# Prompt attention of a hybrid decoder step: weights divided by their sums before their transposition, the sink of mixer B as a column of logits

## What is computed

```python
def sparse_attend(q, k_sel, v_sel, dist, table):           # mixer A
    logits = einsum('btngd,btjnd->btngj', q, k_sel) * HEAD_DIM ** -0.5 + bias
    logits = where(dist >= 0, logits, NEG)
    p = softmax(logits, axis=-1)
    o = einsum('btngj,btjnd->btngd', p, v_sel)

def sink_softmax(logits, sinks):                            # mixer B
    m = maximum(max(logits, axis=-1, keepdims=True), s)
    e = exp(logits - m)
    return e / (sum(e, axis=-1, keepdims=True) + exp(s - m))
```

## Time and profile before

| | |
|---|---|
| median of 3 runs | 2341.65 us (2341.57 to 2344.51) |
| the profiled execution, its own time | 2343.02 us |
| its span, first to last instruction | 2341.2 us |
| mean granted TensorE clock | 0.982 of full |
| busy in the span | PE 96%, PEld 87%, DVE 49%, ACT 18%, POOL 44% |
| prompt attention of mixer A | about 595 to 727 us of the span |
| prompt attention of mixer B | about 1764 to 1844 us of the span |

### The profile page before, as it was taken

How to read it: one execution, slowest core, us unless ns; L and a number is a source line. 1 busy time by engine, 2 the same in 40 slices (tenths; PEclk the granted TensorE clock), 3 DMA queues, 4 the chain that set the end, 5 groups by cost and what they waited for, 6 DMA issues and landing times.

```text
span 2341.2 us, 39794 instructions
## 1 busy us (share of the span) xinstructions
PE 2258.6 (96%) x14801; PEld 2029.8 (87%) x14819; DVE 1137.1 (49%) x1811; ACT 415.4 (18%) x848; POOL 1029.7 (44%) x622
## 2 busy tenths in 40 slices
PE   7999999999888899999999999999999999999997
PEld 6999989959666588999999999999996689999997
DVE  4544522488584546555512555542264465555311
ACT  3101000131554412010000101000015420101002
POOL 4546455414001024555555555555541055555552
PEclk9999999999799999999999999999999899999998
DMA  5435363535003433333223333322350023333221
GB/s 125 99 73 115 78 155 89 114 64 147 10 1 100 130 89 77 86 81 81 78 84 90 82 86 85 81 78 82 94 154 23 1 73 81 81 86 83 79 83 60
DMA packets 378042, 196.33 MB, mean 84 GB/s; under 512 B 66531, under 2 KB 374476, under 8 KB 377932
## 3 DMA queue, kind: packets, MB, share of 16 engines
q1 hardware_dynamic: 366108, 180.79, 31.3%
q10 hardware_dynamic: 11552, 13.71, 2.0%
q0 software_dynamic: 288, 0.56, 0.1%
HBM read 192.23 MB, written 11.64 MB: 87 GB/s over the span
## 4 chain that ended last, share of the span: by engine, by line
PE 61%; DVE 2%; ACTq 0%; ACT 0%; issue 0%; DVEq 0%
PE psum L594 17%; PE psum L597 11%; PE psum L595 10%; PE psum L593 10%; PE psum L596 9%; PE psum L749 1%; PE psum L775 1%; DVE XS L1448 1%; PE psum L745 1%; PE psum L789 1%; ACTq L1200 0%; PE psum L758 0%; DVE squares L1481 0%; PE psum L939 0%; PE psum L938 0%
## 5 line engine op out<-in xcount | busy, mean ns | idle before, releaser
L545 POOL CAST WSP<-WST 128x1024 fp32r<-128x1024 f32 (+1 forms) x305 | 310.5, 1018 | 1250.0 <-PE psum L597 1008.8
L547 POOL TENSOR_TENSOR WSP<-WST,WSP 128x1024 fp32r<-128x1024 f32 (+1 forms) x305 | 709.3, 2326 | 24.5
L594 PE MATMUL psum<-XS,WSP 128*128 128x512 f32 x1672 | 658.4, 394 | 0.0
L593 PE MATMUL psum<-XS,WSP 128*128 128x320 f32 x1672 | 520.4, 311 | 9.5 <-DVE XS L1448 4.3
L597 PE MATMUL psum<-XS,WSP 128*128 128x320 f32 x1672 | 522.7, 313 | 0.0
L595 PE MATMUL psum<-XS,WSP 128*128 128x320 f32 x1672 | 519.2, 311 | 0.0
L596 PE MATMUL psum<-XS,WSP 128*128 128x256 f32 x1672 | 474.0, 283 | 0.0
L596 PEld LDWEIGHTS psum<-XS,WSP 128*128 128x128 f32 x1672 | 314.8, 188 | 71.5
L593 PEld LDWEIGHTS psum<-XS,WSP 128*128 128x128 f32 x1672 | 321.4, 192 | 11.6 <-DVE XS L1448 5.2
L597 PEld LDWEIGHTS psum<-XS,WSP 128*128 128x128 f32 x1672 | 321.5, 192 | 0.0
L594 PEld LDWEIGHTS psum<-XS,WSP 128*128 128x128 f32 x1672 | 314.4, 188 | 0.4
(11 more groups left out here) (325 smaller groups left out, 2595.0 us busy)
## 6 DMA issues: line engine op xcount, KB each, us to landing
WST<-in_ffn_w_gate SPq DMA_DIRECT2D x168, 256.0 KB, 3.9
WST<-in_ffn_w_up SPq DMA_DIRECT2D x168, 256.0 KB, 3.9
WST<-in_ffn_w_down SPq DMA_DIRECT2D x192, 224.0 KB, 3.5
WST<-in_a_w_in SPq DMA_DIRECT2D x28, 256.0 KB, 4.4
kv0A<-in_cache_kv SPq DMA_DIRECT2D x48, 128.0 KB, 2.3
kv2A<-in_cache_kv SPq DMA_DIRECT2D x48, 128.0 KB, 2.3
WST<-in_b_w_in SPq DMA_DIRECT2D x20, 256.0 KB, 4.0
kscr<-in_cache_idx SPq DMA_DIRECT2D x128, 32.0 KB, 2.1
```

Of the source, the lines that this page charges most:

```text
L545: nc.gpsimd.tensor_copy(WSP[s][:, 0, 0:width], WST[s][:, 0:width]).then_inc(w_hi, 1)
L547: nc.gpsimd.tensor_tensor(WSP[s][:, 1, 0:width], WST[s][:, 0:width], WSP[s][:, 0, 0:width].bitcast(F32), ALU.subtract).then_inc(w_split, 1)
L593: mm(front, high, x[:, 0, 0:FRONT], start=first, stop=False)
L594: mm(split, high, x[:, :, FRONT:TOK], start=first, stop=False)
```

## The change

The weights are divided before they are transposed, so that the products with v need no scaling.

- For each unit VectorE takes the reciprocals of its two sums (`factors(u)`, 128x2), queued behind the maximum of unit u + 1. Then the two halves of `p` are multiplied in place by the row's reciprocal: in mixer A by GpSimd (two TENSOR_SCALAR of 128 x nk, the second behind the first), in mixer B by VectorE itself (two TENSOR_SCALAR). `transposed(u)` waits for these (`pn_set`) instead of for the exponentials.
- `row_scales` of TensorE, `scales` of ScalarE, `products` of VectorE and `otok` are gone. The high part is read from the bank by ScalarE (`high_part`), the low part by VectorE (`low_part`), half a tile at a time, in units g = 5 and 7 of a tile and g = 1 and 3 of the next.
- TensorE's order is now `logits(u + 2)`, `values(u - 1)`, `transposed(u)`.
- In mixer B the strip has two columns more (`STRIP["B"]` = 258): the sink and a masked one. They are added to the logits by the strip's matmuls; maximum and exponentials run over nk + 2 columns, and the sink's own steps (L1602, `es`) go.
- `block_diagonal` of mixer A moves from VectorE behind unit 27 to GpSimd behind unit 1: a memset 128x1024 and two copies of 64 x 512.
- GpSimd waits for the last multiplication, no longer for `qk_ps`, before it splits `outA`. In mixer A's sample attention the keys of sample 0 are transposed ahead of the small products (`new_logits`), and wait only for the bank that they write; in mixer B the first key transpositions wait for no evacuation.

```diff
         def _(pool):
+            def block_diagonal(m, ms):
+                pool.wait_ge(acc_evac, at["inA"][1] + A_CHUNKS + RING)
+                nc.gpsimd.memset(m["qbd"][:, :, :], 0.0).then_inc(ms["qbd_clear"], 1)
...
-            pool.wait_ge(MS["A"]["qk_ps"], NQT * GRP)
+            m, ms = mixers["A"], MS["A"]
+            for u, (i, g) in enumerate((i, g) for i in ORDER["A"] for g in range(GRP)):
+                pool.wait_ge(ms["ri_set"], u + 1)
+                for n in range(KVH):
+                    if u or n:
+                        pool.wait_ge(ms["pn_set"], 2 * u + n)
+                    p = m["p"][:, u % 2, n, 0:key_range("A", i)[1]]
+                    nc.gpsimd.tensor_scalar(p, p, m["ri"][:, i, n, g:g + 1], None, ALU.mult).then_inc(ms["pn_set"], 1)
+                if u == 1:
+                    pool.wait_ge(ms["pn_set"], 4)
+                    block_diagonal(m, ms)
+            pool.wait_ge(MS["A"]["pn_set"], 2 * NQT * GRP)
...
         def _(pe):
-                                 m["ri"][:, i, n, g:g + 1].to_broadcast([P, HD]), ident[:, :], start=True, stop=True)
...
-                        pe.wait_ge(ms["p_set"], 2 * u + n + 1)
+                        pe.wait_ge(ms["pn_set"], 2 * u + n + 1)
...
-                        pe.wait_ge(ms["o_evac"], 2 * (r - 1) + g // 4 + 1)
+                        pe.wait_ge(ms["ot_evac"], 2 * (r - 1) + g // 4 + 1)
...
-                for u, (r, i, g) in enumerate(units):
-                    more = u + 2 < len(units)
-                    transposed(u)
-                    if g == GRP - 1:
-                        row_scales(r, i)
-                    elif more:
+                for u in range(len(units)):
+                    if u + 2 < len(units):
                         logits(u + 2)
                     if u:
                         values(u - 1)
-                    if g == GRP - 1 and more:
-                        logits(u + 2)
+                    transposed(u)
                 values(len(units) - 1)
...
         def _(act):
-                    nk = key_range(L, i)[1]
+                    nk = key_range(L, i)[1] + SINK[L]
...
+                def high_part(r, h):
                     i = ORDER[L][r]
+                    act.wait_ge(ms["pv_ps"], GRP * r + 4 * h + 4)
+                    fn(XH[:, 4 * h:4 * h + 4, i * P:(i + 1) * P], bank[6 + h].rearrange("p (g t) -> p g t", g=4), ACT.Copy)\
+                        .then_inc(ms["oh_set"], 1)
...
         def _(dve):
+                def factors(u):
+                    r, i, g = units[u]
+                    dve.wait_ge(ms["p_set"], 2 * (u + 1))
+                    nc.vector.reciprocal(m["ri"][:, i, :, g], m["rs"][:, i, :, g]).then_inc(ms["ri_set"], 1)
+                    if L == "B":
+                        dve.wait_ge(ms["ri_set"], u + 1)
+                        for n in range(KVH):
+                            p = m["p"][:, u % 2, n, 0:key_range(L, i)[1]]
+                            ts(p, p, m["ri"][:, i, n, g:g + 1], None, ALU.mult).then_inc(ms["pn_set"], 1)
...
+                    nc.vector.tensor_reduce(m["nm"][:, i, :, g], PS[u % 2][:, :, 0:nk], AX, ALU.max, negate=True)\
+                        .then_inc(ms["nm_set"], 1)
+                    if u:
+                        factors(u - 1)
+                    if g == 7:
+                        low_part(r, 0)
                     if g == 3 and r:
-                        parts(r - 1)
+                        low_part(r - 1, 1)
                     after(u)
...
+SINK = {"A": 0, "B": 2}
+STRIP = {L: 2 * P + SINK[L] for L in "AB"}
```

More of the change, by code:

```diff
@@ L1237, in prompt_attention @@
                         exps(u + 1)
-                    if L == "A" and r and g == 2:
-                        high_parts(r - 1)
-                    if L == "B" and g == GRP - 2:
-                        act.wait_ge(ms["es_in"], r + 1)
-                        fn(m["es"][:, :, :], m["es"][:, :, :], ACT.Exp).then_inc(ms["es_set"], 1)
                     nk = key_range(L, i)[1]
@@ L1256, in prompt_attention @@
                     after(u)
-                    if g == GRP - 1:
-                        scales(r)
-                if L == "A":
-                    high_parts(NQT - 1)
+                    if g == 5:
+                        high_part(r, 0)
+                    if g == 1 and r:
+                        high_part(r - 1, 1)
+                high_part(NQT - 1, 1)
             def paged_sample_attention(m, ms):
@@ L1558, in prompt_attention @@
                 units = [(r, i, g) for r, i in enumerate(ORDER[L]) for g in range(GRP)]
-                def row_scales(r):
-                    i = ORDER[L][r]
-                    dve.wait_ge(ms["p_set"], 2 * GRP * (r + 1))
-                    rs, ri = m["rs"][:, i], m["ri"][:, i]
-                    if L == "B":
-                        dve.wait_ge(ms["es_set"], r + 1)
-                        steps.done(tt(rs, rs, m["es"][:, :, :], ALU.add))
-                    nc.vector.reciprocal(ri, rs).then_inc(ms["ri_set"], 1)
@@ L1593, in prompt_attention @@
                         between(r)
[L1594 to L1596 removed]
+                    nk = key_range(L, i)[1] + SINK[L]
                     dve.wait_ge(ms["qk_ps"], u + 1)
[L1598 to L1610 removed]
+                    nc.vector.tensor_reduce(m["nm"][:, i, :, g], PS[u % 2][:, :, 0:nk], AX, ALU.max, negate=True)\
[4 more added lines that the diff above has]
+                        low_part(r, 0)
                     if g == 3 and r:
[L1612 removed]
+                        low_part(r - 1, 1)
                     after(u)
[L1614 to L1616 removed]
+                factors(len(units) - 1)
+                low_part(NQT - 1, 1)
             def paged_sample_attention(m, ms):
```

106 lines of the change are left out of this document (29 added, 77 removed).

## The result

The changed kernel takes 2347.39 us in the median of 20 runs (2340.88 to 2354.71), the kernel before, run between them on the same chip, 2343.3 (2338.27 to 2346.68, 20 runs). The ratio is 1.0021, with a 95% interval of 1.0011 to 1.0031: some 5 us slower, where 2332.5 and a ratio of 0.996 were forecast. The profiled execution of the change took 2354.71 us (span 2352.9) and is the slowest of its 20; stages are therefore compared by their own lengths, not by the two ends.

The account below looks back on a forecast made before the run. TensorE was taken to bound mixer B; mixer A begins as a loop of small steps over several engines. A -0.6, clock +1.5 and B -10.0 made -9.1 us: 2333.9 profiled, 2332.5 us median, range 2327 to 2344.

Parts of the forecast that it names:

- A, to the end of tile 0: Mixer A, tile 0: turns of 4.4 us add 8.8 over seven turns, first transposition 1.2 later: +10.0 us.
- A, tiles 1 and 2: Mixer A: tile ends' row scales go, VectorE's queue is what is left, 57.3 plus 1.5 us against 65.2: -6.4.
- A, tile 3: Mixer A, tile 3: two row-scale groups of 2 us and the last product go, one group counted: -2.0 us.
- A, start of the sample part: Mixer A's sample attention: key transpositions now lie beside the last high and low part: -2.2 us.
- A, clock: Mixer A: TensorE, working a smaller part of tile 0, may get 2.4 GHz a few us later: +1.5 us.
- B, first to last transposition: Mixer B: the extra 2.62 us at each of three tile ends is removed, together 7.9 us.
- B, end of the prompt part: Mixer B, last transposition to first key transposition: 4.06 us falls to 1.0, saving 3.1 us.
- B, fill: Mixer B, first unit: reciprocal and multiplications lack cover once: +1.0 us.
- the 1.3 that the prediction had named as a sign of being wrong: Mixer A: a GpSimd multiplication above 1.3 us for 512 would show the forecast wrong.
- The first rival: Mixer A: GpSimd becomes the bound, +13.8 us at the subtraction's rate, 2346.3 us; decides from 2.24 ns per element; chance 0.16.
- 1.5 for imperfect overlap: Mixer A, tiles 1 and 2: 1.5 us added to the 57.3 us of VectorE's queue.
- The third rival: Mixer A: TensorE stays at 1.2 GHz through tile 1, about +8 us, 2340.5, no change; chance 0.10.

Follow-up runs that it names:

- kernel 5: The change, but GpSimd multiplies only the first column of each half in mixer A, leaving other weights undivided; 0.9955 of the kernel before.
- kernel 2: The change in mixer A alone, mixer B taken back to the old functions; 1.0042 of the kernel before.
- kernel 1: The change in mixer B alone, mixer A dividing behind the products as before; 0.9977 of the kernel before.
- kernel 6: The change, with tile 0's reciprocals in mixer A right behind the unit's own maximum, multiplications still on GpSimd; 0.9977 of the kernel before.
- kernel 7: The change, with tile 0's reciprocals in mixer A right behind the unit's own maximum and its multiplications on VectorE; 0.9973 of the kernel before.
- the filling: 11 idle transpositions before mixer B's last two products with v; added to the change in mixer B alone, 0.9966 of the kernel before.

## Why the prediction was wrong, point by point

| term of the sum | forecast | profile of the change |
|---|---|---|
| A, to the end of tile 0 | +10.0 | +14.1 |
| A, tiles 1 and 2 | -6.4 | -2.4 |
| A, tile 3 | -2.0 | +1.3 |
| A, start of the sample part | -2.2 | -2.1 |
| A, clock | +1.5 | inside the rows above |
| B, first to last transposition | -7.9 | -7.2 |
| B, end of the prompt part | -3.1 | -2.2 |
| B, fill | +1.0 | +1.6 |
| B, sample part | 0 | +3.7 (none to 3.7) |

- **The step that failed is the price of GpSimd's multiplication.** "The multiplication has one tensor in and one out, so I take the CAST's rate: 0.27 us for 128 keys, 0.61 for 512". It took 0.605 and, unhindered, 1.57, above the 1.3 that the prediction had named as a sign of being wrong. Over 64 multiplications that is 71.7 us, where the forecast's rate gives 28. Kernel 5 is the test: its pair takes 0.66 us, as forecast for tile 0, and there the sum came out, 35.5 us to the transposition of tile 0's last unit beside 25.5, +10.0. A third of what kernel 5 saves lay on the path; a third of the 44 us between 28 and 71.7 is some 15 (an estimate from kernel 5), where all of A came out 10.1 longer than forecast (+11.0 for +0.9). So the forecast's other terms for A were together some 4 to 5 us too dear, and hid a part of the miss.

  An operation's count of inputs didn't tell its cost; the row nearest in shape was the wrong neighbour, and the bound on the other side was the nearer one. The first rival, with its 2.24 ns per element as the point from which it decides (2.22 by its own sum), was the case that came, with a chance of 0.16 where the only row against it was the CAST. That its time came so close, 2346.3 for 2347.39, is luck in part: it stands for A +14.7 and B -10.0, and kernels 2 and 1 measured +9.8 and -5.4; and it put half of the price on the path, where kernel 5 shows a third. The Trainium skill (GPSIMD Engine Reference, sections 3.1 and 4.1) has one-input work at roughly line rate and two-input work at 2.6 cycles per element; the CAST agrees with the first, the multiplication at 2.5 ns doesn't, and the measurement decides.
- **Tile 0.** The chain was right, step by step; 0.66 us for the pair was 1.30, and the turn 4.89 for 4.4. What I did not ask is whether that chain was needed. I took the reciprocal's place behind the next maximum as given and priced it; kernels 6 and 7 show that in the early place the turn is 3.54 us, as before the change, with either engine. Of the 10.3 us by which u1 to u8 grew, the move alone takes 9.8, VectorE in the old place 4.8, the price at one element 4.1.
- **Tiles 1 and 2.** The steady turn was forecast at 2.85 and is 2.77; VectorE's queue is the turn there, as said. The failed part is "1.5 for imperfect overlap": the turns with a low part take 4.4 to 5.2 us and not 3.5 to 4.0, since VectorE waits in them for ScalarE's high part, behind a transposition that waits for GpSimd. With one element to multiply (kernel 5) this stretch takes 54.9 us, -10.3, more than forecast: this is where the sum was too dear, and the price took it back.
- **Tile 3.** The multiplication beside TensorE's 4.0 us was expected to be hidden, and from the tile's second transposition on it is (turns of 4.0 us and less). The first turns pay, in part through the lock between VectorE and GpSimd (below), which I had looked for in the small search steps and not in the cut's long scan.
- **Mixer B.** Mechanism right, each term 0.6 to 0.9 us too hopeful: -7.8 for -10.0. Missing was any term for the clock behind it, +3.7 in this profile; in the times B alone gave 5.4 us, and 8.0 with the filling. I called the copy and products at the end 1.0 us of waiting and did not ask what TensorE's idleness does to the stage behind.
- **The rest.** The third rival (1.2 GHz through tile 1) did not come as told: the clock rose at 638.8 us, before at 620.6, at the end of tile 0 in both, and fell again for 10 us in all in tile 1, before for 7. Kernel 6 has turns of 3.54 us at 1.2 GHz, so the lower clock is not what lengthens tile 0's turns. The block-diagonal layout on GpSimd and `outA`'s later weights cost nothing that the profile shows, as forecast (sample part 110.6 us in both).

## What to carry to other kernels

Before an engine's price is argued over, ask what the step is queued behind: here a reciprocal placed one instruction later put GpSimd's 1.3 us per unit into the turn of the loop, and moving it ahead was worth 10 us, where the faster engine in the old place gave 8. Where a price has no row, let the rival's point of decision, and not the likeliest neighbour, say how much chance it gets. And a stage that ends in short waits can hand a slower TensorE to the next one: look at the granted clock behind the place where work was removed.

## What the runs showed of the hardware

- **GpSimd, multiplication by a column, f32:** 0.605, 0.926 and 1.246 us for 128, 256 and 384 elements, 1.57 for 512, and 0.29 for one in kernel 5 (two in 0.66). That is 2.5 ns per element and 0.29 fixed, more than its subtraction of two tensors, 2.2 ns. VectorE takes 0.48 for two of 128.
- **VectorE's scan locks GpSimd out.** The timeline of VectorE and GpSimd in the change, at the start of tile 3:

```profile
705.83 2.30 DVE L1894 TENSOR_TENSOR_SCAN squares<-scwA 128x1032 f32<-128x1032 f32 x1
...
705.94 5.22 POOL L587 TENSOR_SCALAR pA<-pA,riA 128x512 f32<-128x512 f32 x2 [2.42 <-DVE riA L1556]
...
717.48 1.57 POOL L587 TENSOR_SCALAR pA<-pA,riA 128x512 f32<-128x512 f32 x1 [2.65 <-DVE riA L1556]
```

  Two multiplications take 5.22 us beside the scan, where one alone takes 1.57 and two 3.23: 2 us of the scan's 2.30 are lost to GpSimd. The multiplication that starts 0.1 us behind the scan took 3.56 us in all seven profiles that have it, and in kernel 5, where it has one element, 2.28 us instead of 0.28, until the scan's end. It is the mirror of the earlier trace rows, where VectorE waited for GpSimd.
- **TensorE's clock at a stage's end.** Three waits of 0.8 to 0.9 us with some 0.5 us of weight loads between them went with a fall to 1.2 GHz in 11 of 12 profiles, of 3.4 or of 13.7 us; 11 idle transpositions in the last two of them kept 2.4 GHz in 4 of 4. The long falls are those that began earlier; why they begin earlier in one profile than in another no run here shows.
